# A hybrid decoder step on one core: earlier pages and tables, query tiles spread over the expert units, the samples' choice moved, two accumulators

## The reference, cut to what matters

```python
def indexer_topk(iq, iw, ik, q_pos, n_sel):          # samples: ik is gathered from the pages of cache_idx_k
    s = jnp.einsum('bthd,bsd->bths', iq, ik) * IDX_DIM ** -0.5
    score = jnp.einsum('bth,bths->bts', iw, jax.nn.relu(s))
    _, idx = lax.top_k(jnp.where(k_pos <= q_pos, score, -jnp.inf), n_sel)

def peer(h, p):                                      # n tokens: two blocks of 128 prompt tokens, then 8 samples
    q = (h @ p['peer_wq']).reshape(n, PEER_HEADS, 2, PEER_HALF)
    s = jnp.einsum('nhcd,chkd->nhck', q, p['peer_keys'])
    s1, i1 = lax.top_k(s[:, :, 0], PEER_TOPK)        # 16 of 128, for each of 8 heads and both halves
    s2, i2 = lax.top_k(s[:, :, 1], PEER_TOPK)
    cand_s = (s1[..., :, None] + s2[..., None, :]).reshape(n, PEER_HEADS, 256)
    cand_i = (i1[..., :, None] * 128 + i2[..., None, :]).reshape(n, PEER_HEADS, 256)
    top_s, pos = lax.top_k(cand_s, PEER_TOPK)        # 16 of 256
    eidx = jnp.take_along_axis(cand_i, pos, axis=-1)
    g = jax.nn.softmax(top_s, axis=-1)
    act = jax.nn.gelu(jnp.einsum('nd,nhkd->nhk', h, p['peer_u'][eidx]))
    return jnp.einsum('nhk,nhkd->nd', g * act, p['peer_v'][eidx])
```

## Time and profile before

| | |
|---|---|
| median of three runs | 1525.81 us |
| the profiled execution's own time | 1524.46 us |
| its span, first to last instruction | 1522.8 us |
| busy: PE, DVE, ACT, POOL | 1254.8, 870.9, 602.0, 398.8 us |
| moved by DMA | 391.14 MB, of which gathers and other POOL transfers 287.34 MB |
| the chain that ended last, largest entry | transfers of `pe_uv`, 20% of the span |

### The profile page before, as it was taken

The page is one execution under the profiler, slowest core; times in us unless marked ns, Lnnn a source line. Parts: engine busy times, 40 slices in busy tenths (PEclk is TensorE's granted clock), DMA queues, the critical chain, the costliest instruction groups (busy, mean ns, idle before and its releaser), DMA issues. The chain is left out here.

```text
span 1522.8 us, 17756 instructions
## 1 busy us (share of the span) xinstructions
PE 1254.8 (82%) x4972; PEld 772.8 (51%) x4972; DVE 870.9 (57%) x2346; ACT 602.0 (40%) x1566; POOL 398.8 (26%) x510
## 2 busy tenths in 40 slices
PE   5968999999676877879989989787776788788787
PEld 4846668777555555668867555332222322222221
DVE  1015449999274336760126765889989654454453
ACT  1125237878474314510014343433433444444443
POOL 1331002220022110000002424443646433333341
PEclk8978999999786898989999999999999899999999
DMA  4543223323199450054138988999999699999997
GB/s 151 169 157 113 84 70 119 116 98 109 51 328 343 147 191 1 5 204 188 61 124 319 377 326 349 423 421 421 418 421 421 280 421 422 421 422 422 422 422 317
DMA packets 77071, 391.14 MB, mean 257 GB/s; under 512 B 11384, under 2 KB 22168, under 8 KB 39616
## 3 DMA queue, kind: packets, MB, share of 16 engines
q0 software_dynamic: 43168, 287.34, 46.2%
q1 hardware_dynamic: 33088, 101.32, 18.8%
q10 hardware_dynamic: 736, 1.56, 0.3%
HBM read 378.43 MB, written 11.60 MB: 256 GB/s over the span
## 5 line engine op out<-in xcount | busy, mean ns | idle before, releaser
L1689 PE MATMUL pe_acc<-pe_uv,pe_dg 128*128 128x512 f32 (+1 forms) x1056 | 513.3, 621 | 132.7 <-ACT pe_dg L1759 129.5
L1940 DVE CUSTOM_DVE_ANT_0 pe_uv<-pe_uv,pe_hnat 128x1024 f32<-128x1024 f32 x264 | 321.8, 1222 | 207.8 <-DMA pe_uv<-d_uv,pe_idx 196.5
L1689 PEld LDWEIGHTS pe_acc<-pe_uv,pe_dg 128*128 128x128 f32 (+1 forms) x1056 | 185.7, 190 | 456.0 <-ACT pe_dg L1759 283.2
L1810 POOL DMA_INDIRECT pe_uv<-d_uv,pe_idx x256 | 285.4, 1115 | 404.9 <-PE pe_acc L1689 366.8
L180 PE MATMUL pi_ps<-xn,pi_w 128*128 128x264 f32 x944 | 227.2, 398 | 9.5 <-PEq L86 9.5
L180 PEld LDWEIGHTS pi_ps<-xn,pi_w 128*128 128x128 f32 x944 | 182.9, 197 | 42.4 <-issue 11.3
L1753 ACT ACTIVATE pe_gl<-pe_a 128x1 f32<-128x1 f32 x264 | 53.0, 201 | 305.0 <-DVE pe_a L1940 301.8
L1759 ACT ACTIVATE pe_dg<-cst,pe_w 128x128 f32<-128x128 f32 x256 | 102.8, 401 | 8.3
L1756 ACT ACTIVATE pe_w<-pe_gl,pe_gw 128x1 f32<-128x1 f32 x256 | 75.4, 295 | 20.4
L1636 PE MATMUL pq_ps<-hN,pq_w 128*128 128x264 f32 x256 | 61.5, 401 | 5.6 <-DMA pq_w<-d_wq 5.6
L1792 POOL COPY pe_hrep<-hN 128x128 f32<-128x128 f32 x8 | 1.9, 295 | 236.7 <-DVE hN L1947 236.7
(11 more groups left out here) (284 smaller groups left out, 1676.0 us busy)
## 6 DMA issues: line engine op xcount, KB each, us to landing
pi_w<-d_w_in SPq DMA_DIRECT2D x71, 512.0 KB, 3.3
mg_w<-d_w_ab SPq DMA_DIRECT2D x8, 1536.0 KB, 6.6
ss_h<-d_state SPq DMA_DIRECT2D x8, 1024.0 KB, 5.9
o_ssm_s<-ss_h SPq DMA_DIRECT2D x8, 1024.0 KB, 6.9
pq_w<-d_wq SPq DMA_DIRECT2D x16, 512.0 KB, 7.6
lg_w<-d_w_in SPq DMA_DIRECT2D x10, 512.0 KB, 6.5
paged<-d_ck POOLq DMA_DIRECT2D x32, 128.0 KB, 5.7
paged<-d_ck SPq DMA_DIRECT2D x32, 128.0 KB, 6.1
```

Of the source, the lines that this page charges most:

```text
L1689: mm = pe.matmul(acc[0:m, 4 * half:4 * half + 4, :], lhsT, uv[:, r, D_MODEL + half * 512:D_MODEL + (half + 1) * 512], start=False, stop=Fa ...
L1810: pool.indirect_dma_start(uv[:, r, :], None, k.d_uv[:], bass.IndirectOffsetOnAxis(ap=src, axis=0)).then_inc(gathered[r], 16)
L1940: dve.tensor_tensor_reduce(uv[:, r, 0:D_MODEL], uv[:, r, 0:D_MODEL], hnat[:, n, :], 1.0, 0.0, ALU.mult, ALU.add, a[:, r:r + 1]).then_inc(d ...
```

## The change

**Pages and tables.** `IK_FIRST` falls from 44 to 36. In `prepare_attention` the 14 pages 36 to 49 are loaded by SP, in six small loops behind its six weight loads, with a semaphore of their own (`ik_by_sp`); POOL loads the last 14. The three tables are loaded by ACT at the start of `project_attention`, into buffers that live longer. The first four visits' key pages (16 pages of 128 KB) are loaded by POOL at the end of its program in `attend_prompt`, with a semaphore for each visit; in `attend_sample` SP and POOL begin with visit 4, so SP's first state loads follow its two tables directly.

**Expert stage.** From the third unit on one query tile (not two) is computed ahead of every fifth unit (3, 8, ... 38), and a head's scores two units after its second tile. The choice of the second tile is spread over 56 units in place of 40; the samples' choice moves to units 128 to 191, which are in the second tile. The second tile accumulates in `pe_ph`, which the transposed tokens used before, so PE starts it eight units before the first tile ends with the residual and goes on; ACT reads an accumulator out after the second unit of the tile that follows. The units of the second tile are written out instead of looped.

```diff
-IK_FIRST = 44
+IK_FIRST, IK_SECOND = 36, 50
+KV_SLOTS, KV_PAGES = 4, 4
...
@@ project_attention, scalar
             act.dma_start(pj.old[:], k.d_old[:]).then_inc(pj.c_loaded, 16)
+            act.dma_start(k.gqk[:], k.d_gqk[:]).then_inc(k.tables_loaded, 16)
+            act.dma_start(k.rel[:], k.d_rel[:]).then_inc(k.tables_loaded, 16)
+            act.dma_start(k.hot[:], k.d_hot[:]).then_inc(k.tables_loaded, 16)
...
@@ prepare_attention
-            sp.dma_start(gqk[:], k.d_gqk[:]).then_inc(c_loaded, 16)
-            sp.dma_start(rel[:], k.d_rel[:]).then_inc(c_loaded, 16)
-            sp.dma_start(hot[:], k.d_hot[:]).then_inc(c_loaded, 16)
...
-            for n in tiles:
+            pages = shares(range(IK_FIRST, IK_SECOND), len(tiles))
+            for i, n in enumerate(tiles):
                 k.proj.load(sp, n + WSLOTS)
+                load_indexer_pages(sp, k, pages[i][0], pages[i][-1] + 1, k.ik_by_sp)
...
-            pe.wait_ge(c_loaded, 48)
+            pe.wait_ge(k.tables_loaded, 48)
...
-            load_indexer_pages(pool, k, IK_FIRST, TS * PAGES)
+            load_indexer_pages(pool, k, IK_SECOND, TS * PAGES, k.ik_loaded)
...
@@ attend_prompt, gpsimd
             for n in tiles:
                 k.proj.tails(pool, n)
+            kv = k.paged[:].rearrange("p (g i n) -> p g i n", g=KV_SLOTS, i=KV_PAGES)
+            for visit in range(KV_SLOTS):
+                for i in range(KV_PAGES):
+                    at = (2 * i + visit % 2) * PAGES + visit // 2
+                    page = pool.value_load(k.pages[0:1, at:at + 1], min_val=0, max_val=k.n_pool - 1)
+                    pool.dma_start(kv[:, visit, i:i + 1, :], k.d_ck[bass.ds(page, 1)].rearrange("a s n -> s a n")
+                                   ).then_inc(k.kv_first[visit], 16)
...
@@ attend_sample
+            if visit < NG:
+                pe.wait_ge(k.kv_first[visit], 16 * GP)
+                return
...
             for b in range(ssd.SLOTS):
-                load(sp, by_sp, 0, b)
                 ssd.load(sp, b)
...
-            for visit in range(ssd.SLOTS, 2 * VK):
+            for visit in range(NG, 2 * VK):
...
@@ peer
+        accs = (acc, ph, acc)
...
-        TURNS = ((0, 1), (1, 3), (3, 5), (5, 7), (7, 12), (12, LOOPS[0]))
+        SPANS = ((0, RING), (RING, 3 * RING), (3 * RING, 5 * RING), (5 * RING, 7 * RING), (7 * RING, 14 * RING),
+                 (PER, PER + 8 * RING))
...
-        queries_at = {1 + h - AHEAD: h for h in range(AHEAD, PH)}
+        query_at = {3 + 5 * i: 2 * AHEAD + i for i in range(2 * (PH - AHEAD))}
+        scores_at = {u + 2: n // 2 for u, n in query_at.items() if n % 2}
...
+            residual(0)
+            for n in range(3):
+                for i in range(LOOPS[n] * RING):
+                    if n == 0 and i in query_at:
+                        query(query_at[i])
+                    if n == 0 and i in scores_at:
+                        scores(scores_at[i])
+                    mix(n, i)
+                    if n < 2 and i == LOOPS[n] * RING - RING:
+                        residual(n + 1)
...
@@ peer, scalar
+                    weigh(n, i)
+                    if n == 0 and i in query_at:
+                        query(query_at[i])
+                    if n == 0 and i in scores_at:
+                        scores(scores_at[i])
+                    if n and i == 1:
+                        finish(n - 1)
```

More of the change, by code:

```diff
@@ L1297, in _ @@
         def _(pool):
-            for visit in range(2 * VK):
+            for visit in range(NG, 2 * VK):
                 load(pool, by_pool, 1, visit)
@@ L1674, in _, with residual @@
             scores(AHEAD - 1)
-            for n, (t0, m) in enumerate(TILES):
-                if n:
-                    pe.wait_ge(y_read, n)
+            def residual(n):
+                t0, m = TILES[n]
+                if n == 2:
+                    pe.wait_ge(y_read, 1)
+                if n == 1:
+                    pe.wait_ge(h_read, 3)
                 for c in range(KD):
-                    pe.matmul(acc[0:m, c, :], k.xT[:, c, t0:t0 + m], k.ident, start=c % 4 == 0, stop=False,
+                    pe.matmul(accs[n][0:m, c, :], k.xT[:, c, t0:t0 + m], k.ident, start=c % 4 == 0, stop=False,
@@ L1682, in _ @@
                               skip_group_check=True)
-                def steps(i):
-                    for r in range(RING):
-                        pe.wait_ge(diagonal, BEFORE[n] + i * RING + r + 1)
-                        lhsT = dg[:, r, :] if n < 2 else dg[:, r, 0:TS]
-                        for half in range(2):
-                            mm = pe.matmul(acc[0:m, 4 * half:4 * half + 4, :], lhsT,
-                                           uv[:, r, D_MODEL + half * 512:D_MODEL + (half + 1) * 512],
-                                           start=False, stop=False, skip_group_check=True)
-                        mm.then_inc(accumulated, 1)
@@ L1693, in _, with mix @@
-                if n == 0:
-                    for i in range(LOOPS[0]):
-                        if i in queries_at:
-                            queries(queries_at[i])
-                            scores(queries_at[i])
-                        steps(i)
-                elif n == 1:
-                    with pe.Fori(0, LOOPS[n]) as i:
-                        steps(i)
-                else:
-                    steps(0)
+            def mix(n, i):
+                at, m = BEFORE[n] + i, TILES[n][1]
+                r = at % RING
+                pe.wait_ge(diagonal, at + 1)
+                lhsT = dg[:, r, :] if n < 2 else dg[:, r, 0:TS]
+                for half in range(2):
+                    mm = pe.matmul(accs[n][0:m, 4 * half:4 * half + 4, :], lhsT,
+                                   uv[:, r, D_MODEL + half * 512:D_MODEL + (half + 1) * 512],
+                                   start=False, stop=False, skip_group_check=True)
+                mm.then_inc(accumulated, 1)
@@ new lines, in weigh @@
+            def weigh(n, i):
+                at = BEFORE[n] + i
+                r = at % RING
+                act.wait_ge(dotted, at + 1)
+                act.activation(gl[:, r:r + 1], a[:, r:r + 1], ACT.Gelu_apprx_tanh).then_inc(gelued, 1)
+                act.wait_ge(gelued, at + 1)
+                g = gw[:, n, i:i + 1] if n < 2 else gws[:, i:i + 1]
+                act.activation(wt[:, r:r + 1], gl[:, r:r + 1], ACT.Copy, scale=g).then_inc(weighed, 1)
+                act.wait_ge(weighed, at + 1)
+                out, mask = (dg[:, r, :], k.ident) if n < 2 else (dg[:, r, 0:TS], k.own_h)
+                act.activation(out, mask, ACT.Copy, scale=wt[:, r:r + 1]).then_inc(diagonal, 1)
@@ L1781, in _ @@
                     act.wait_ge(y_out, 16 * n)
-                act.activation(y[0:m, :], acc[0:m].rearrange("p c d -> p (c d)"), ACT.Copy).then_inc(y_read, 1)
+                act.activation(y[0:m, :], accs[n][0:m].rearrange("p c d -> p (c d)"), ACT.Copy).then_inc(y_read, 1)
                 act.wait_ge(y_read, n + 1)
                 act.dma_start(k.o_y[t0:t0 + m, :], y[0:m, :]).then_inc(y_out, 16)
+            act.wait_ge(chosen, 1)
+            for n in range(3):
+                if n == 2:
+                    act.wait_ge(moved, 32)
+                for i in range(LOOPS[n] * RING):
+                    for c, (first, end) in enumerate(SPANS):
+                        if BEFORE[n] + i == end:
+                            exponents(c + 1)
+                            act.wait_ge(chosen, c + 2)
+                    weigh(n, i)
[5 more added lines that the diff above has]
+                        finish(n - 1)
+            finish(2)
             act.wait_ge(y_out, 48)
@@ L1932, in weights, with dot @@
                                   ).then_inc(chosen, 1)
[L1934 to L1938 removed]
+            def dot(n, i):
+                at = BEFORE[n] + i
+                r = at % RING
+                dve.wait_ge(gathered[r], (at // RING + 1) * 16)
+                if at >= RING:
                     dve.wait_ge(gelued, at - RING + 1)
```

144 lines of the change are left out of this document (57 added, 87 removed).

## The result

The changed kernel takes 1500.01 us, median of four runs (1497.89 to 1503.75), against 1523.38 for the kernel before on the same occasions: a ratio of 0.9837 with a 95% interval of 0.9806 to 0.9869. By the ratio that is some 25 us faster. The forecast was 1483 in a range of 1468 to 1502; the direction came as forecast, the gain was six tenths of it.

A forecast was written before the change was run, and what follows sets the result against it. The expert stage was taken as limited by gathers, PE or DVE in turn, with DMA at 420 GB/s from 1200 us. Gains 12 + 4 + 15 + 12 - 1 = 42 us from 1524.5 gave 1483, range 1468 to 1502.

The forecast's parts named there:

- Pages and tables: First half: fewer indexer pages on POOL and tables loaded earlier win 12 us, bounds 9.8 to 13.2.
- a rival that had a chance of 0.13: Second tile or `attend_prompt` barrier late: gathers stretched to 2.71 us, 1496 us; or page loads stretched, up to 1499; chance 0.13.
- the tables' 2.7 us: `prepare_attention`: first product came 2.7 us after the start, behind table `hot`; with tables already there it starts with the stage.
- Key pages and state: Start of `attend_sample`: four visits' pages loaded early and state sooner win 4 us, bounds 2 and 5.5.
- the bound of 16 us: End of `attend_prompt`: if POOL's 16 page loads were stretched like gathers, they would end 16 us late; zero taken.
- Queries in single tiles: Expert stage, first 40 units: single query tiles win 15 of 19.0 us lost, bounds 5 and 19.
- I leave 4 us: Allowance for hand-overs at units 8, 24 and 40, with no slack between PE and DMA: 4 us.
- Samples' choice in the second tile: Expert stage: moving this choice and spreading the second tile's over 56 units wins 12 us, bounds 5 and 13.
- So 1 us remains: Second tile: DVE about 7.5 us late over 16 to 18 units, ring slack some 10 us, so 1 us of loss remains.
- the old kernel's 2.2 us: Window 1100 to 1183 us: 2.2 us lost, taken as the most that the second tile's choice cost at this pace.
- Two accumulators, units written out: Change of tiles and second tile: accumulators worth nothing by themselves, though the gap goes only with both edits; written-out units zero.
- the slower rival: Written-out second tile: instruction fetches compete with transfers; from 0.33 us a unit the gain is gone, about 1533 at 0.4; chance 0.03.

## Why the prediction was right, and where not

The time lies in the stated range, at its slow end, and outside the 1470 to 1491 that I gave to the forecast itself. It lies where the rivals stood, and the range holds it because it held them: the larger miss is the mechanism of a rival that had a chance of 0.13, gathers held behind DVE in the second tile.

*Pages and tables: mechanism right, size too small.* I took 12 us in bounds of 9.8 to 13.2; the stage began 11.4 us sooner and was 5.1 us shorter, 16.5 in all. That POOL's loop held the barrier is shown by the run with 44 pages. The barrier took 0.85 us (85.66 to 86.51), the short end of the two that I gave. The term that was too small is the tables' 2.7 us: it counted PE's wait and not the clock that PE has behind it (0.50 in the first 5 us before, 1.00 now). That the first half still came out at 15.5 us of 16 is in part luck: `time_steps` and the chunked scan each took 3.2 us longer in this execution than before; in the other runs with early pages they took 20.2 to 24.5 and 88.1 to 90.6 us, where this one has 23.6 and 91.0.

*Key pages and state: size right, not resolved.* 4 us were forecast, 150.0 - 145.7 = 4.3 seen in the profiled pair; the runs scatter by as much. POOL's page loads were not stretched, 0.54 us each, and done 7.5 us before the barrier: the bound of 16 us was not touched. The Trainium skill's rule (SBUF — State Buffer, "SBUF: two separate sides"), which I had weighed against these loads, did not show here, with VectorE (DVE) busy for 16.46 of these 19.00 us; whether any of its operations there was of the two-port kind that the rule is about, no run shows.

*Queries in single tiles: mechanism right, one term mis-sized.* PE was busy for 105.38 us over the first 40 units against my 104.7, and the waits of POOL, 13.65 us and the like, fell to 4 or 5, with one of 7.5. That 7.5 is over the 5 us that I had named as a sign of being wrong. The failed term is "I leave 4 us" for the hand-overs. They cost 5.5 + 6.1 us. The reason is a consequence of the edit that I had not followed: ACT reads a query tile out in its own order, behind the weights of units 23 and 38, and waits there until PE, several units late, has made it; the exponentials of units 24 and 40 stand behind that. The run with early exponentials gave 6.8 us of the stage back, and the transfers' limit was reached.

*Samples' choice in the second tile: wrong.* The step that failed is "So 1 us remains". I had summed DVE's lateness and held it against the ring's slack. DVE's lateness cost little. The run with early exponentials and 128 partitions has as many pieces of the same length behind as many dots, and in the 20 us in which its large pieces end it loses 2.3 us of transfers, at 372 GB/s:

```profile
1225.00:1245.00 20.00, 15.92 (x36) 6.40 (x35) 17.22 (x24) 8.09 (x27) 12.18 (x9) 1.00 0.98 372
```

What the sum left out is POOL: a gather's issue is held while DVE works on pieces of 8 partitions and dots in turn. I had seen the stretched issue of 2.41 us and priced it among the rivals, at 13.4 us over 64 units (1496 us). Its place and form were others: the stretched issues themselves cost nothing (421 GB/s in the window's third row), one held issue cost 15 us. And I had misread the old kernel's 2.2 us, on which I rested: the window of 1100 to 1183 us holds the samples' choice, on 8 partitions, not the second tile's. That one ran before it and lost nothing, but on 128 partitions:

```profile
993.00:1095.00 102.00, 77.17 (x160) 27.62 (x159) 97.01 (x284) 38.34 (x123) 48.41 (x40) 1.00 1.01 421
```

*Two accumulators, units written out: right.* Units 192 to 255 took 157.1 us against 156.6; the slower rival is out. At the change of tiles (PE's residual at 1124.95 us, its first product into `pe_ph` at 1142.98, ACT's read-out at 1145.23) the transfers stayed at 421 GB/s from 1125 to 1160 us.

## What to carry to other kernels

Before moving small-partition work of VectorE (DVE) beside gathers that GpSimd (POOL) issues, look at the length of the issues beside such work, not only at its mean: a stretch that costs nothing at 2.4 us can become a hold of 20 us when the pieces get longer. Work whose length is set by the elements of a row can be done on all 128 partitions at almost no cost in time (2.29 us for a large piece where it was 2.27), which cured it here, as did a short break in each second unit. When a producer's work is cut into pieces, follow the consumer's program too: what waits in order behind each piece's read-out moves with it. And a wait of TensorE (PE) at a stage's start costs more than its length when the granted clock has fallen in it: 3.1 us of wait came with 2.0 us of slower products here.
